# Quarters of the first product groups one row tile earlier among the first transposes, and one VectorE subtraction placed ahead of another at the start of the block products

## The reference, cut to what matters

```python
def rms_norm(x, g):
    y = xf * lax.rsqrt(jnp.mean(xf * xf, axis=-1, keepdims=True) + EPS)
    return (y * g).astype(x.dtype)

proj = h @ w_in                       # h: tokens x 1024, w_in: 1024 x D_IN
(..., gates) = jnp.split(proj, ...)   # the last 4*1024 columns are the gates
gate = jax.nn.sigmoid(gates.reshape(bt, t, N_BRANCH, D_MODEL))
```

## Time and profile before

| | us |
|---|---|
| median of 3 runs | 2177.02 (2176.74, 2177.02, 2178.87) |
| the profiled execution | 2176.39 |
| its span in the trace | 2174.6 |
| PE busy | 2151.3 (99%) |
| PEld busy | 2035.9 (94%) |
| DVE busy | 1243.4 (57%) |
| POOL busy | 1103.8 (51%) |
| ACT busy | 696.5 (32%) |

### The profile page before, as it was taken

The page is one execution under the profiler, slowest core; times in us unless marked ns, Lnnn a source line. Parts: engine busy times, 40 slices in busy tenths (PEclk is TensorE's granted clock), DMA queues, the critical chain, the costliest instruction groups (busy, mean ns, idle before and its releaser), DMA issues. The chain is left out here.

```text
span 2174.6 us, 34482 instructions
## 1 busy us (share of the span) xinstructions
PE 2151.3 (99%) x13883; PEld 2035.9 (94%) x13883; DVE 1243.4 (57%) x1855; ACT 696.5 (32%) x1152; POOL 1103.8 (51%) x1329
## 2 busy tenths in 40 slices
PE   8999999999999999999999999999999999999998
PEld 7999999999999999999999999889999998888877
DVE  8522221799755435543453365658566667788775
ACT  5444442333231111242222121335333333333332
POOL 4444443778442333232234454710556658789880
PEclk9999999999999999999999999999999999999999
DMA  5233332121221121132242555323354446644432
GB/s 188 91 100 101 100 101 84 40 59 50 64 90 47 34 61 53 43 86 82 81 132 96 189 177 180 128 73 109 121 174 151 135 152 225 209 134 130 142 117 83
DMA packets 212787, 239.89 MB, mean 110 GB/s; under 512 B 14434, under 2 KB 156838, under 8 KB 212619
## 3 DMA queue, kind: packets, MB, share of 16 engines
q1 hardware_dynamic: 209745, 227.38, 33.0%
q0 software_dynamic: 2304, 8.91, 1.1%
q10 hardware_dynamic: 578, 1.38, 0.2%
HBM read 169.37 MB, written 68.64 MB: 109 GB/s over the span
## 5 line engine op out<-in xcount | busy, mean ns | idle before, releaser
L2202 POOL TENSOR_TENSOR w_lo<-w_raw,w_hi 128x256 fp32r<-128x256 f32 x490 | 380.6, 806 | 413.6 <-ACT w_hi L1719 413.0
L1166 PE MATMUL acc<-h_hi,w_hi 128*128 128x368 f32 (+2 forms) x1696 | 552.5, 326 | 0.5 <-issue 0.5
L1168 PE MATMUL acc<-h_hi,w_lo 128*128 128x368 f32 (+2 forms) x1696 | 546.5, 322 | 0.0
L1167 PE MATMUL acc<-h_lo,w_hi 128*128 128x368 f32 (+2 forms) x1696 | 546.0, 322 | 0.0
L1166 PEld LDWEIGHTS acc<-h_hi,w_hi 128*128 128x128 f32 x1696 | 318.5, 188 | 5.3 <-issue 4.0
L1167 PEld LDWEIGHTS acc<-h_lo,w_hi 128*128 128x128 f32 x1696 | 318.7, 188 | 0.0
L1168 PEld LDWEIGHTS acc<-h_hi,w_lo 128*128 128x128 f32 x1696 | 318.5, 188 | 0.0
L1719 ACT ACTIVATE w_hi<-w_raw 128x1024 fp32r<-128x1024 f32 (+2 forms) x162 | 141.5, 875 | 341.3 <-PE acc L1168 215.2
L2202 POOL TENSOR_TENSOR w_lo<-w_sum,w_hi 128x256 fp32r<-128x256 f32 x156 | 125.9, 832 | 134.0 <-ACT w_hi L1719 129.0
L1166 PE MATMUL pz<-t_op,w_hi 128*128 128x272 f32 x648 | 186.7, 288 | 0.3 <-POOL w_lo L2202 0.3
L1167 PE MATMUL pz<-t_op,w_hi 128*128 128x272 f32 x648 | 186.7, 288 | 0.0
(11 more groups left out here) (509 smaller groups left out, 4914.9 us busy)
## 6 DMA issues: line engine op xcount, KB each, us to landing
w_raw<-in_w_in SPq DMA_DIRECT2D x70, 512.0 KB, 4.1
a_raw<-down_operands SPq DMA_DIRECT2D x49, 512.0 KB, 3.8
gate_values<-staging SPq DMA_DIRECT2D x29, 544.0 KB, 3.7
gsig<-gate_values SPq DMA_DIRECT2D x29, 544.0 KB, 3.6
down_operands<-v_sums SPq DMA_DIRECT2D x14, 1024.0 KB, 4.4
w_raw<-in_w_up SPq DMA_DIRECT2D x18, 512.0 KB, 5.1
b_raw<-branch_outputs POOLq DMA_DIRECT2D x16, 544.0 KB, 5.5
w_raw<-in_w_branch SPq DMA_DIRECT2D x16, 512.0 KB, 4.7
```

The source lines that it names most:

```text
L1166: pe.matmul(out, lh, rh, start=first, stop=False, skip_group_check=more)
L1167: pe.matmul(out, lh, rl, start=False, stop=False, skip_group_check=more)
L1168: return pe.matmul(out, ll, rh, start=False, stop=last, skip_group_check=more)
L2202: return pool.tensor_tensor(out, x, y, op)
```

## The change

Two places. In TensorE's list the turns and the quarters are ordered anew: tiles 0 to 3 are turned alone; from tile 4 on, two quarters stand before each tile. So the pair (0,0,0), (0,0,1) stands before tile 4 where it stood before tile 5, and so on, and the pair (0,1,0), (0,1,1) now stands before tile 8 and before `turn_params` and `phase_end`. Six quarters are left behind the phase end where there were eight. In VectorE's list `lead_op(1)` stands before the low part of token operand t = 1, where it stood after it. No instruction is added or removed.

```diff
-            for i in range(NT - 3):
+            quarters = [(u, g, q) for g in range(2) for u in range(2) for q in range(4)]
+            for i in range(4):
                 turn_tokens(i)
-            for i in range(4):
-                for q in range(2):
-                    early(i // 2, 0, 2 * (i % 2) + q)
-                turn_tokens(NT - 3 + i)
+            for i in range(4, NT + 1):
+                early(*quarters[2 * i - 8])
+                early(*quarters[2 * i - 7])
+                turn_tokens(i)
             turn_params()
             phase_end(pe, "pe", 1, wait=False)
-            for u in range(2):
-                for q in range(4):
-                    early(u, 1, q)
+            for u, g, q in quarters[2 * (NT - 3):]:
+                early(u, g, q)
...
                 for n, t in ((2, 1), (1, 2), (3, 0), (4, 3)):
-                    if n == 1:
+                    if n == 2:
                         lead_op(1)
+                    elif n == 1:
                         lead_op(2)
                         g_sums(0, (2,))
```

## The result

The changed kernel takes 2184.18 us in the median of nine runs (2182.34 to 2186.50). The kernel before, run beside it, takes 2179.20 (2176.74 to 2182.19, nine runs). The ratio is 1.0022, 95% interval 1.0013 to 1.0030, so the change costs 2.8 to 6.5 us, 4.8 at the ratio. The forecast was 2183.0, +6.0, with a range of 2180.8 to 2185.0. Over 33 other runs, before had a median of 2179.47 (2175.30 to 2182.28); the 2177.02 that I started from was at the low end of its own spread. The profiled execution of the changed kernel took 2183.79, its span 2182.0 for 2174.6.

The account below looks back on a forecast made before the run. PE was taken as busy 99% of the span, with DVE's chain feeding it without slack at e = 4. DVE's delay 2.56 + pause 1.75 = 4.3, plus clock 1.7, made +6.0 us: 2183.0, range 2180.8 to 2185.0.

Parts of the forecast that it names:

- The first quarter cannot use the idle time: Before tile 4: the quarter waits for DVE's later half of tile 2, starts at 19.06, idle grows to 2.32 us.
- Delay of DVE's chain by edit 1: Reordered turns and quarters: tile 8 is turned later, so DVE's first long sum starts 2.56 us later, at 35.20.
- The wait before unit 2: PE, ready at 47.71, waits some 1.5 us for lead_low(2), which ends at 49.18.
- The pause of edit 2: With lead_op(1) moved ahead, DVE stands still 1.75 us for ScalarE's copy g_high(1).
- Waits at e = 2 and e = 4: PE waits 0.9 us at e = 2 for its bank and about 1.7 us at e = 4 for operand 4.
- The sum without the clock: At e = 4 and after: DVE's late start and its pause, 2.56 + 1.75, reach PE as 4.3 us.
- The bound of 2.6: Other end of the lateness at e = 4, if GpSimd's operand 4 is not slowed beside DVE: 2.6 us, not 4.3.
- The clock, 1.7 us: Idle time before tile 4: granted clock falls to half, costing 1.7 us within 0 to 2.8; chance 0.60.
- The waits of PE: Over the whole span PE's waits were put at a few microseconds in all, two of them where the change acts.
- that the clock stays: Rival: no fall of the clock before tile 4, so +4.3 us, 2181.3; chance 0.30.
- that the lateness is taken up later: Rival: DVE's lateness reaches PE only in part or a later wait returns some; +0.5 to +2.6 us; chance 0.07.
- that the idle time is filled: Rival: the idle time before tile 4 is filled, PE 1.7 us earlier, faster at 2175.3 us; chance 0.03.

Follow-up runs that it names:

- after_filled: The changed kernel with 20 transposes of the identity put before the first quarter, in the idle time; 2182.91 us, ratio 1.0017.
- quarters_only: The changed kernel with lead_op(1) back in its old place, so only TensorE's list is reordered; 2182.52 us, ratio 1.0015.
- the two filled kernels: The changed kernel with 20 and the kernel before with 14 transposes of the identity in their idle time; 2182.91 and 2178.71 us.
- hi_first_filled: The kernel before with operand 4 made by DVE, eight h_hi matmuls before tile 4's turn, and eight identity transposes before tile 3's; 2177.34 us, ratio 0.9989.
- before_again: The kernel before, unaltered, traced once more; 2180.09 us in a single run.
- before_op4: The kernel before with the low part of weight operand 4 made by DVE instead of GpSimd; 2178.96 us, ratio 1.0002.
- after_again: The changed kernel, unaltered, traced once more; 2182.80 us in a single run.
- hi_first_op4: The kernel before with operand 4 made by DVE and eight matmuls that need only high token parts before tile 4's turn; 2177.68 us, ratio 0.9992.

## Why the prediction was right

It was right in its range, its sign and the steps of the chain; the term of the clock was charged to the change without being shown to belong to it, and single sizes were off as follows.

- **The first quarter cannot use the idle time.** Forecast 19.06 with 2.32 us of idle time; measured 19.10 with 2.31.
- **Delay of DVE's chain by edit 1, 2.56 us.** Without a fall of the clock it is 19.76 - 17.06 = 2.70 (after_filled), and PE's own lateness at unit 2 is 0.71 where 0.55 was forecast (50.50 less its wait of 1.50, 32.29 from tile 3, for 31.58). quarters_only carries its delay through unchanged (45.63 us from DVE's start to e = 6).
- **The wait before unit 2, 1.5 us.** Measured 1.51, 1.50 and 1.50.
- **The pause of edit 2, 1.75 us.** Measured 1.62 in the changed kernel, 1.84 alone.
- **Waits at e = 2 and e = 4, 0.9 and 1.7.** Measured 0.54 and 1.52. I had the two as overlapping, which holds: they follow from one late chain.
- **The sum without the clock, 4.3.** Measured 4.34 at e = 6 in after_filled, and 4.20 between the medians of the two filled kernels. The bound of 2.6 without GpSimd's contention was too low: with operand 4 taken off GpSimd only 0.48 us came back, as the next pair's sum has the same origin.
- **The clock, 1.7 us.** That a fall here delays DVE's chain, and that this passes on in full, is shown: 1.2 to 2.5 us at DVE's start, the same at e = 6, and none with the gap filled. Two parts of the argument did not hold. I tied the fall to the idle time growing from 1.72 to 2.32 us, past the 2.1 at which it fell near 1826; but it fell inside that idle time in two of four traces of the new order, after it in one, and before tile 3, where nothing had changed, in one. And I charged the whole of it to the change although I took one run of before as such a fall myself. The kernel before loses the clock in two of four traces and, by the mean clock of the timed runs, about as often as the new order (57% and 68% at 0.997 or less). What is left of the term is the difference in frequency times 1.2 to 2.5 us: 0.6 to 1.3 by the traces' two of four and four of four, 0.1 to 0.3 by the timed runs. With 4.3 this makes 4.4 to 5.6, where 4.8 (2.8 to 6.5) was measured and 6.0 forecast. The interval holds 4.3 and 6.0 alike, so the times do not test this term. My last paragraph named this as the way to be wrong.
- **The waits of PE, "a few microseconds in all".** They come to about 16 us over the whole span, 5.0 of them before the first tile is turned. The ones where the change acts were read rightly.
- **The level.** 2184.18 is 1.2 above the forecast although the change cost 1.0 less by the medians, as before's own median was 2.2 us above the three runs I had. The two misses have opposite signs, so it is in part luck that the time came out so near.

Of the rivals: that the clock stays gives 4.34, which is most of what was measured; that the lateness is taken up later is against the equal waits at e = 6; that the idle time is filled could not happen in this order, and hi_first_filled shows that even when it is filled the next limit, DVE, leaves 0.2 us of it.

## What to carry to other kernels

Before filling an engine's idle time with a step, compare the semaphore value that the step waits for with that of the step it is put in front of: if it is later, the idle time grows and everything behind moves. When the bound engine looks busy 99% of the time, look for the second chain that feeds it. Here PE's own lateness was 0.7 us, and what reached the end was the lateness of VectorE's chain, whose start hangs on the last transpose before the phase end. An operand moved ahead of another in an in-order list needs its producer to be ahead too: `lead_op(1)` stood waiting 1.6 us for a copy that stands behind other work in ScalarE's list. And before a fall of the clock is charged to a change, look in several executions of both kernels where it begins: one that begins ahead of the first changed instruction is not the change's.

## What the runs showed of the hardware

Around the first transposes, where TensorE works in short pieces between idle times of 1.3 to 2.3 us, the granted clock went from 1.00 to 0.50 in eight of the ten traces without added transposes, for 3.4 or 6.8 us, and at moments from 0.5 us before the turn of tile 3 to 4.3 us after it. Two traces of the same kernel differ in this. While the level was down, 368-column matmuls started 0.31 us apart instead of 0.17, and a fall cost 0.42 to 0.44 of the time that TensorE worked in it. Transposes of the identity, whose results nobody reads, went with a level of 1.00 in each of the three traces that had them. The work after the first 80 us took 2095 to 2099 us by execution. At its idle time of 3.2 us near 1830 the clock fell for 6.8 us in four traces (before, before_again, before_op4, after_again), for 3.4 us in six, and not at all in three (the changed kernel's first, after_filled, hi_first_op4). Those three have waits for DVE in its place; the changed kernel's first trace:

```profile
1832.84 0.50 PE L1166 MATMUL acc<-w_hi,a_op 128*128 128x512 f32 x1 [3.23 <-POOL w_lo L2202]
1836.55 0.50 PE L1668 MATMUL pz<-w_hi,packs_d 128*128 128x512 f32 x1 [0.71 <-DVE x_s L2545]
1840.50 0.50 PE L1166 MATMUL pz<-w_hi,a_op 128*128 128x512 f32 x1 [1.39 <-DVE x_s L2545]
```

There the idle time is the 3.2 us of before, the clock stays, and the engine waits 2.1 us more for DVE. The first row of the group of products that follows, in before and then in the changed kernel:

```profile
1841.85 0.39 PE L1166 MATMUL pz<-w_c,a_op 128*128 128x512 f32 x1
```

```profile
1847.45 0.39 PE L1166 MATMUL pz<-w_c,a_op 128*128 128x512 f32 x1
```

It stands 14.63 us after the end of the idle time in before, with 5.6 us of work at half clock (1841.85 - 1827.22), and 14.61 in the changed kernel, with none (1847.45 - 1832.84). So the fall cost nothing there: the slower matmuls filled time in which TensorE waits for DVE otherwise. A fall of the clock can cost almost half of the work in it or nothing, and one profiled execution tells little about differences of 2 us in this kernel unless they are read stage by stage.
